# The third block's head projections in three fp32r passes over halves kept in DRAM

## The reference

```
mod = (silu(c) @ w_mod + b_mod)            # six vectors of 1024; also for the context
h = rmsnorm(x, norm1_w) * (1 + scale) + shift
pq, pff, pfb, pi, pg, ... = split(h @ w_in)   # parts of 1024 columns
# heads of 128: q = pq, values = pi, two forget gates from pff and pfb, output gate from pg
k_f, log_f = 1 - sigmoid(pff), log(clip(sigmoid(pff), 1e-6, 1))     # and backwards from pfb
o = gated linear attention(q, k_f, v, log_f, forwards) + the same backwards with k_b, log_b
y_hg = (rmsnorm(o) * silu(pg)) @ w_hg_out
```

## Time and profile before

| | us |
|---|---|
| median of 3 runs (3785.17 to 3787.79) | 3785.26 |
| the profiled execution | 3788.17 |
| its span, first to last instruction | 3786.4 |
| mean granted clock of TensorE | 0.963 of full speed |

### The profile page before, as it was taken

How to read it: one execution, slowest core, us unless ns; L and a number is a source line. 1 busy time by engine, 2 the same in 40 slices (tenths; PEclk the granted TensorE clock), 3 DMA queues, 4 the chain that set the end, 5 groups by cost and what they waited for, 6 DMA issues and landing times. The chain is left out here.

```text
span 3786.4 us, 42191 instructions
## 1 busy us (share of the span) xinstructions
PE 3564.5 (94%) x15836; PEld 2702.9 (71%) x15836; DVE 1619.4 (43%) x2764; ACT 1064.8 (28%) x1875; POOL 1526.6 (40%) x873
## 2 busy tenths in 40 slices
PE   8999999999989699999999998999899899699998
PEld 7887977777746477777746886877555578578886
DVE  4832013333222314444322104342588778757741
ACT  2112022222221523333422001146466510222111
POOL 6764643323202423333204663663000056356664
PEclk9999999999989889999999998999999899899999
DMA  4322221111132211111244321332111122122321
GB/s 151 100 99 73 95 67 46 50 45 51 50 100 89 85 42 59 55 57 56 68 149 145 112 95 59 109 101 71 45 51 50 34 89 93 52 78 95 101 95 56
DMA packets 83212, 295.19 MB, mean 78 GB/s; under 512 B 9185, under 2 KB 10721, under 8 KB 82882
## 3 DMA queue, kind: packets, MB, share of 16 engines
q1 hardware_dynamic: 80352, 286.34, 22.8%
q10 hardware_dynamic: 1970, 3.67, 0.3%
q0 software_dynamic: 688, 2.49, 0.2%
HBM read 289.32 MB, written 2.10 MB: 77 GB/s over the span
## 5 line engine op out<-in xcount | busy, mean ns | idle before, releaser
L584 POOL TENSOR_SCALAR arena_r<-ring 128x1024 fp32r<-128x1024 f32 x430 | 463.3, 1078 | 2112.3 <-PE psum L596 1387.4
L594 PE MATMUL psum<-arena_r,arena_r 128*128 128x512 f32 (+2 forms) x3120 | 1240.8, 398 | 44.2 <-POOLq L587 18.4
L595 PE MATMUL psum<-arena_r,arena_r 128*128 128x512 f32 (+2 forms) x3120 | 1208.8, 387 | 0.0
L596 PE MATMUL psum<-arena_r,ring_r 128*128 128x512 f32 (+1 forms) x3088 | 1197.7, 388 | 0.0
L586 POOL TENSOR_TENSOR ring_r<-ring,arena_r 128x1024 fp32r<-128x1024 f32 x430 | 1053.5, 2450 | 72.8 <-issue 18.2
L594 PEld LDWEIGHTS psum<-arena_r,arena_r 128*128 128x128 f32 x3120 | 595.9, 191 | 185.6 <-issue 36.1
L595 PEld LDWEIGHTS psum<-arena_r,arena_r 128*128 128x128 f32 x3120 | 596.0, 191 | 122.6 <-issue 9.4
L596 PEld LDWEIGHTS psum<-arena_r,ring_r 128*128 128x128 f32 x3088 | 585.3, 190 | 119.9
L1092 DVE SCALAR_TENSOR_TENSOR arena<-arena,con,psum 128x512 f32<-128x512 f32 x64 | 47.8, 747 | 558.0 <-PE psum L1038 558.0
L2246 PE MATMUL psum<-arena,ring 128*128 128x512 f32 x512 | 234.5, 602 | 14.6 <-ACT arena L2321 14.5
L2246 PEld LDWEIGHTS psum<-arena,ring 128*128 128x128 f32 x512 | 94.5, 194 | 114.3 <-issue 114.3
(11 more groups left out here) (379 smaller groups left out, 4305.3 us busy)
## 6 DMA issues: line engine op xcount, KB each, us to landing
ring<-in_weights SPq DMA_DIRECT2D x534, 512.0 KB, 3.3
arena<-in_x_t SPq DMA_DIRECT2D x8, 256.0 KB, 6.2
out_t<-arena SPq DMA_DIRECT2D x8, 256.0 KB, 2.2
arena<-in_w_ck POOLq DMA_DIRECT2D x1, 1024.0 KB, 9.3
arena<-in_w_cv POOLq DMA_DIRECT2D x1, 1024.0 KB, 11.3
arena<-in_ln_bc ACTq DMA_DIRECT2D x1, 1024.0 KB
arena<-in_ctx_t ACTq DMA_DIRECT2D x1, 1024.0 KB, 7.1
arena<-in_pos SPq DMA_DIRECT2D x2, 256.0 KB, 4.3
```

The costliest lines, as they stand in the source:

```text
L584: nc.gpsimd.tensor_scalar(hi_part(t), src, 1.0, 1.0, ALU.mult, ALU.mult)
L594: nc.tensor.matmul(out, w_hi, a_hi, start=start, stop=False)
L595: nc.tensor.matmul(out, w_hi, a_lo, start=False, stop=False)
L596: return nc.tensor.matmul(out, w_lo, a_hi, start=False, stop=stop)
```

## The change

The 32 tiles of the head projections are no longer loaded in the third block. They come into the ring in the second block's attention, one after every second slot (`with_puts`, jobs named "put"; 32 of them, the last seven behind slots 51, 53, 55, 57, 59, 61 and 63, which hold groups of w_mod). POOL halves such a tile as any other. SP writes both halves to a new DRAM array `put_dram`. PE does nothing with the tile: after the product of an odd slot it waits until both writes have landed, and then raises `w_used` by one with a drain, which frees the slot and the high buffer. In SP's program the two writes of tile t stand behind the load of tile t + 5.

In the third block's heads, POOL issues 64 loads of halves from `put_dram` into the ring, with semaphores `put_back` of their own. `project_half` uses two ring slots, high and low half, and does `three` on n_hi and n_lo. It raises `w_used` by two. Counts of `w_used` that others wait for are changed to match, and `arrivals` keeps `w_in` counts right for tiles behind the 64.

```diff
+def with_puts(slots):
+    out = []
+    for n, job in enumerate(slots):
+        out.append(job)
+        if n % 2:
+            out.append(("put", n // 2))
+    return out
...
+        put_dram = nc.dram_tensor("put_dram", (4 * KT, 2, P, 1024), F32, kind="Internal").ap()
...
         def load_tiles(sp, t0, n):
-            for t in range(t0, min(t0 + n, n_tiles)):
-                if t >= RING:
+            for t in range(t0, min(t0 + n, n_tiles + 8 * KT)):
+                if t >= RING and not 0 <= t - halves_at[0] < 8 * KT:
                     sp.wait_ge(w_used, t - RING + 1)
+                at = t - halves_at[0]
+                if 0 <= at < 8 * KT:
+                    continue
                 sp.dma_start(ring[:, t % RING * 1024:(t % RING + 1) * 1024],
-                             weights[t]).then_inc(w_in[t % RING], 16)
+                             weights[t if at < 0 else t - 8 * KT]).then_inc(w_in[t % RING], 16)
+                if t - 5 in put_by:
+                    j, done = put_by[t - 5]
+                    sp.wait_ge(w_split, split_no[t - 5] + 1)
+                    sp.dma_start(put_dram[j, 0], hi_part(t - 5).bitcast(F32)).then_inc(done, 16)
+                    sp.dma_start(put_dram[j, 1], lo_part(t - 5).bitcast(F32)).then_inc(done, 16)
...
                             tile_columns(pe, at[job], 7, h_hi, h_lo)
+                        if n % 2:
+                            pe.wait_ge(put_done, 32 * (n // 2 + 1))
+                            pe.drain().then_inc(w_used, 1)
                         pe.wait_ge(pt_done, n + 1)
...
             @block.gpsimd
             def _(pool):
                 halve_tiles(pool, T0, H0 - T0)
+                for t in range(H0, END):
+                    pool.wait_ge(w_used, t - RING + 1)
+                    pool.dma_start(ring_r[t % RING][:, 0:1024],
+                                   put_dram[(t - H0) // 2, (t - H0) % 2]).then_inc(put_back[t % RING], 16)
...
-                    t = H0 + 4 * hd + PART[part]
+                    t = H0 + 2 * (4 * hd + PART[part])
                     b = PART[part] % 2
                     if half == 0:
-                        pe.wait_ge(w_in[t % RING], 16 * (t // RING + 1))
+                        for i in (t, t + 1):
+                            pe.wait_ge(put_back[i % RING], 16 * ((i - H0) // RING + 1))
                         bank_take(pe, b)
+                    w_hi, w_lo = (lo_part(i).rearrange("p (b m) -> p b m", m=P) for i in (t, t + 1))
                     for k in range(4 * half, 4 * half + 4):
-                        last = nc.tensor.matmul(psum[:, b], slot(t % RING)[:, k], hn[:, k], start=(k == 0),
-                                                stop=(k == KT - 1))
+                        last = three(psum[:, b], w_hi[:, k], w_lo[:, k], n_hi[k], n_lo[k], k == 0, k == KT - 1)
                     if half:
-                        last.then_inc(w_used, 1)
+                        last.then_inc(w_used, 2)
```

More of the change, by code:

```diff
@@ L555, in to_split, with arrivals @@
                 splits[0] += 1
+        put_dram = nc.dram_tensor("put_dram", (4 * KT, 2, P, 1024), F32, kind="Internal").ap()
+        put_by, halves_at = {}, [n_tiles]
+        def arrivals(t):
+            return 16 * (t // RING + 1 - (KT if t >= halves_at[0] + 8 * KT else 0))
         def load_tiles(sp, t0, n):
-            for t in range(t0, min(t0 + n, n_tiles)):
-                if t >= RING:
+            for t in range(t0, min(t0 + n, n_tiles + 8 * KT)):
+                if t >= RING and not 0 <= t - halves_at[0] < 8 * KT:
                     sp.wait_ge(w_used, t - RING + 1)
+                at = t - halves_at[0]
+                if 0 <= at < 8 * KT:
+                    continue
                 sp.dma_start(ring[:, t % RING * 1024:(t % RING + 1) * 1024],
-                             weights[t]).then_inc(w_in[t % RING], 16)
+                             weights[t if at < 0 else t - 8 * KT]).then_inc(w_in[t % RING], 16)
[4 more added lines that the diff above has]
+                    sp.dma_start(put_dram[j, 1], lo_part(t - 5).bitcast(F32)).then_inc(done, 16)
         def hi_part(t):
@@ L714, in mod_group @@
                 t = t0 + q
[L715 removed]
+                pe.wait_ge(w_in[t % RING], arrivals(t))
                 for kk in range(2):
@@ L1183, in hybrid_block @@
             pre, slots, post = hybrid_jobs()
-            jobs = pre + slots + post
+            jobs = pre + with_puts(slots) + post
             at, t = {}, T0
+            put_done = sem("h_put_done")
             for job in jobs:
@@ L1189, in hybrid_block @@
                     to_split(t, 1)
+                if job[0] == "put":
+                    put_by[t] = job[1], put_done
                 t += 4 if job[0] == "mod" else 1
             END = t
+            halves_at[0] = END + 3 * KT
             x = tiles(0, KT)
@@ L2009, in recurrent_heads @@
             H0 = T0 + 8
-            END = H0 + 32
+            END = H0 + 64
             to_split(T0, H0 - T0)
@@ L2020, in recurrent_heads @@
             v_in, mask_in = sem("gla_v_in"), sem("gla_mask_in")
+            put_back = [sem(f"gla_put_back{i}") for i in range(RING)]
             @block.sync
@@ L2316, in gates @@
                     t = PART[part]
-                    act.wait_ge(w_used, H0 + 4 * hd + t + 1)
+                    act.wait_ge(w_used, H0 + 8 * hd + 2 * t + 2)
                     if t == 0 and hd:
@@ L2330, in query @@
                 def query(hd):
-                    act.wait_ge(w_used, H0 + 4 * hd + 3)
+                    act.wait_ge(w_used, H0 + 8 * hd + 6)
                     nc.scalar.activation(q_s[:, hd % 2], psum[:, 0], ACT.Copy).then_inc(bk_free[0], 1)
@@ L2335, in gate_silu @@
                 def gate_silu(hd):
-                    act.wait_ge(w_used, H0 + 4 * hd + 4)
+                    act.wait_ge(w_used, H0 + 8 * hd + 8)
                     nc.scalar.activation(g_s[:, hd % 2], psum[:, 1], ACT.Silu).then_inc(bk_free[1], 1)
@@ L3164, in host @@
     pre, slots, post = hybrid_jobs()
-    ws = [mod[4 * m:4 * m + 4] if c == "mod" else kind[c][m:m + 1] for c, m in pre + slots + post]
+    w3 = a["w_in_3"][0]
+    kind["put"] = blocks(np.concatenate([w3[:, i * D + m * P:i * D + (m + 1) * P] for m in range(KT) for i in (1, 2, 0, 4)],
+                                        axis=1))
+    ws = [mod[4 * m:4 * m + 4] if c == "mod" else kind[c][m:m + 1] for c, m in pre + with_puts(slots) + post]
     gl = w[:, kv + 1536 + D:c0]
@@ L3185, in host @@
     part = [w[:, i * D:(i + 1) * D] for i in range(9)]
-    heads = np.concatenate([part[i][:, m * P:(m + 1) * P] for m in range(KT) for i in (1, 2, 0, 4)],
-                           axis=1)
     gates = np.concatenate([part[i][:, m * P:(m + 1) * P] for m in range(KT) for i in (1, 2)], axis=1)
@@ L3200, in host @@
     mixed = np.concatenate(mixed + [kind["c"][5:8]])
-    third = [blocks(gates), wide_blocks(part[3]), blocks(heads),
+    third = [blocks(gates), wide_blocks(part[3]),
              mixed, blocks(a["w_cv_out_3"][0]), blocks(a["w_out_3"][0]),
```

5 lines of the change are left out of this document (2 added, 3 removed).

## The result

| | us |
|---|---|
| before, median | 3785.93 |
| after, median of 4 (3829.29 to 3840.5) | 3831.15 |
| ratio after to before | 1.0124, 95% interval 1.0106 to 1.0141 |
| the profiled execution of after | 3829.29 |
| its span, and mean granted clock | 3827.6, 0.955 |

The change makes the kernel 45 us slower; I had forecast 24. The two profiled spans differ by 3827.6 - 3786.4 = 41.2 us, because the profiled execution of after is its fastest and that of before is 2 us above its median. The 41.2 us are what the two traces can explain.

The account below looks back on a forecast made before the run. PE, busy 94% of the span, was taken as the bound; heads -13, drains +9, stalls +21 and clock +7 gave +24 on 3788.17, 3812, or 3809 as median; own range 3790 to 3828, wider range 3778 to 3842.

Parts of the forecast that it names:

- Heads, -13: Third block's heads: three-pass half projections save 4.4 us in head 0 and 9 us over seven heads; range 4.4 to 32.
- Returning loads, 0: Heads: the 64 loads of halves on POOL's queue have 41 us to land, so they cost nothing.
- The starved-heads rival: Heads: POOL's loads go one at a time at 8.6 us, adding 196 us, some 4005 in all; chance 0.03.
- the Trainium skill's rule: Heads: descriptors of a POOL-issued DMA can't be written while DVE runs in its two-port mode, so loads would be delayed.
- 25 puts outside w_mod hidden: Plain attention slots: writes, POOL's 113 us of extra work and loads are hidden behind PE's tiles, 5 us to spare.
- Drain, +9: Plain attention slots: PE's drain at each of 25 puts costs 0.35 us, 9 us in all; bounds 0 and 12.
- Stalls, +21: Seven puts behind w_mod slots: PE waits about 3.0 us each for late writes, 21 us; bounds 5 and 49.
- the second at 9.5 to 10.4: w_mod slots: a put's second write lands 9.5 to 10.4 us into the group; PE wants it at 6.95.
- The estimate by the Trainium skill in the prediction: w_mod slots: at 2.0 us plus bytes at 436 GB/s, three transfers land at 9.2; stall 2.2, 16 us for seven.
- Clock, +7: Behind the seven w_mod stalls: PE's matmuls run at a lower clock, 7 us in all; bounds 0 and 19.
- I take 1 us each: Clock loss per 3.0 us stall, set between matmuls taking 6.10 us after 4.5 us idle and 3.67 after 2.33.
- dear stalls: w_mod slots: rival with stalls of 5 us, each costing 2.66 of clock; +50 us in all, 3835; chance 0.18.

Follow-up runs that it names:

- alone: The change's heads with no puts, both half loads fetching the plain weight tile, against the kernel before: 3774.05 us, ratio 0.9965.
- the run with 1.7 us waits: The changed kernel with the writes of the seven w_mod puts issued behind the load four tiles further on instead of five: 3798.3 us, ratio 1.0031.

## Why the forecast was right in direction and half the size

- **Heads, -13:** right in the sum (-13.3 in the trace; -12.6 alone) and in the reason for most of it: the waits before the masked copies went to 0.19, the wait before the states gave back 0.6 us, where I had 0.5, and the period of the middle heads came out at 41.1 to 41.7. The sum is also helped by luck. I cut the heads at an instruction that DVE has once a head (L2437, L2475). Ahead of the first the change won 5.6 us where I had 4.4, since a half took 2.82 us and not 2.93. Of the seven periods five won 0.8 to 1.4 us each, as I had it (1.3). One won 3.9, the one that holds the 4.5 us wait of the earlier trace rows, and the last lost 1.4. Behind them 0.8 us were lost. I had none of these three.
- **Returning loads, 0:** right. They landed in 4.2 us (median of 64, longest 7.9), beside DVE at 82%, and each was in at least 17 us before PE used it. The starved-heads rival, and the Trainium skill's rule behind it, had no effect that shows here.
- **25 puts outside w_mod hidden:** right, no wait at all. **Drain, +9:** too high; 0.18 us each, 4.7 for the 25. I had added the end of the last matmul, the release and the weight load behind it. The trace has the next weight load start 0.10 us behind that end with a drain and 0.07 us ahead of it without one, a difference of 0.17 us.
- **Stalls, +21:** the place, the count, SP's times and the releaser were right, the size was not: 4.2 us each instead of 3.0, 29.6 in all. The step that failed is "the second at 9.5 to 10.4". I let the two writes follow the loads like loads, 1.3 to 1.7 us apart. The lower half landed 6.0 to 7.4 us after its issue in these slots, against 3.9 in the 25 others (median). From trace to trace, the later the writes stand in the burst of loads that the group's releases set off, the slower the lower half lands: 6.8, 5.9, 5.4 and 4.4 us (medians of seven) behind the load five, four, three and two tiles on. Why a write fares so among loads no run settles; writes from a queue other than SP's were not tried. The estimate by the Trainium skill in the prediction, a stall of 2.2 us, was lower still; its section is on DMAs that GpSimd issues, and these are SP's.
- **Clock, +7:** the largest error, and the second step that failed: "I take 1 us each". It is 18.4, or 20.0 with slot 63's value products, against the upper bound of 19 that I gave. That is 2.6 us a wait, the full price I had read from an idle of 4.5 us. At 4.2 us a wait is like that row; at the forecast 3.0 it might have been less, as the run with 1.7 us waits suggests. So the clock's error follows perhaps in part from the stall's; no run has waits of 3 us.

With the measured terms, -13.3 + 4.7 + 29.6 + 1.3 (seven drains, which I had left out) + 18.4 + 0.5 for the rest = +41.2, the difference of the spans. The measured 3831 lies outside the forecast's own range, 3790 to 3828. The case that came nearest is the one I called dear stalls, at 0.18: 4.2 us each instead of 5, and the clock's price as it says. Against it I wrote that 5 us needs writes slower than loads. They were: of 1900 to 2000 us the writes landed in 5.8 and 6.9 us, the loads in 4.3 (medians).

## What to carry to other kernels

Here a wait was decided by where the transfer stood in its queue's program, and not by how much was transferred: two loads' distance in SP's order turned +45 us into -9. When a stall lands on TensorE, price it twice, once for its length and once for the clock behind it, and take the second from a row with the same idle time (the row of 4.5 us gave 2.66, the seven waits of 4.2 us took 2.6 on the mean). Where the size of the stall is uncertain, the clock's price moves with it, so both belong in one case and not in separate terms with separate midpoints.

## What the runs showed of the hardware

- Seven waits of TensorE of 4.2 us (mean) came with 2.6 us each of lower clock over the kernel before; the matmuls right behind them were slow in six of seven. With waits of 1.7 us it was 0.6 us each, and four of seven. 3.7 us of matmuls in the gap took that cost away, though 1.1 us of waiting remained on the mean.
- A 512 KB write to DRAM landed in 2.7 us (upper half) and 3.9 (lower half, issued 0.4 us behind) in plain slots, and in 6.0 and 6.8 among the loads of a w_mod group.
- A drain of TensorE between a tile in three passes and fp32 products cost 0.18 to 0.20 us.
- 64 loads of 512 KB from POOL's queue landed in 4.2 us (median; longest 7.9) beside DVE at 82%.
- The w_mod groups lose 1.6 to 1.7 us now and then at a lower granted clock without TensorE having been idle for more than 0.4 us at a time; their number varied from 0 to 5 of 12 between kernels that are the same in that stretch or nearly so.
